# The softmax's row factors leave attention as rows in DRAM and are multiplied into the gates in the merge stage

## The reference

```python
logits = jnp.where(mask, scores + bias, -jnp.inf)     # 8 heads of width 64
p = jax.nn.softmax(logits, axis=-1)
att = jnp.einsum('bhqk,bkhd->bqhd', p, v)
y_b = att * jax.nn.silu(gbf)
merged = (gates[:, :, 0] * (y_a @ w_up_a) + gates[:, :, 1] * (y_b @ w_up_b)
          + gates[:, :, 2] * (y_c @ w_up_c))
out = merged @ w_out
return layer_norm(ALPHA * x + out, ln_g, ln_b)
```

## Time and profile before

| | |
|---|---|
| median of 3 timed runs | 1953.57 us (1952.46 to 1955.21) |
| profiled execution | 1956.44 us, its span 1954.8 us, mean TensorE clock 0.993 |
| TensorE busy | 1916.7 us (98%), 10560 matmuls |
| VectorE, ScalarE, GpSimd busy | 1125.0 us (58%), 708.7 us (36%), 435.1 us (22%) |
| attention | about 607 to 1577 us |
| merge | 1577 us to the end, a block each 44.6 us |

### The profile page before, as it was taken

The page is one execution under the profiler, slowest core; times in us unless marked ns, Lnnn a source line. Parts: engine busy times, 40 slices in busy tenths (PEclk is TensorE's granted clock), DMA queues, the critical chain, the costliest instruction groups (busy, mean ns, idle before and its releaser), DMA issues. The chain is left out here.

```text
span 1954.8 us, 30551 instructions
## 1 busy us (share of the span) xinstructions
PE 1916.7 (98%) x10560; PEld 1625.1 (83%) x10560; DVE 1125.0 (58%) x2142; ACT 708.7 (36%) x1090; POOL 435.1 (22%) x548
## 2 busy tenths in 40 slices
PE   7999999999999999999999999999999989999998
PEld 6878887888886888888888788888888878999997
DVE  4563235654244655646556665565655568777676
ACT  3121113021033554555555655455555541111110
POOL 1927940498000000000000000000000002222322
PEclk9999999999999999999999999999999989999999
DMA  6224225322432142241513515133142286555542
GB/s 187 65 91 117 89 86 193 66 97 109 138 120 87 56 124 68 66 125 48 138 54 89 186 50 139 54 89 109 48 136 66 87 262 208 167 174 170 174 118 87
DMA packets 105592, 221.69 MB, mean 113 GB/s; under 512 B 11000, under 2 KB 56744, under 8 KB 101928
## 3 DMA queue, kind: packets, MB, share of 16 engines
q1 hardware_dynamic: 92912, 165.61, 26.8%
q0 software_dynamic: 12608, 55.19, 10.2%
HBM read 155.09 MB, written 65.08 MB: 113 GB/s over the span
## 5 line engine op out<-in xcount | busy, mean ns | idle before, releaser
L1447 PE MATMUL g_ps<-x_hi,w_lo 128*128 128x512 f32 x768 | 309.7, 403 | 0.0
L1447 PE MATMUL g_ps<-x_hi,w_hi 128*128 128x512 f32 x768 | 308.2, 401 | 0.0
L1361 DVE TENSOR_TENSOR pt_lo<-t_ps,pt_hi 128x512 fp32r<-128x512 f32 (+2 forms) x320 | 191.7, 607 | 134.3 <-ACT pt_hi L1269 132.9
L1447 PE MATMUL g_ps<-x_lo,w_hi 128*128 128x512 f32 x768 | 228.1, 412 | 3.7 <-PEq L1484 2.7
L697 PE MATMUL tile_ps<-x_hi,w_hi 128*128 128x512 f32 x736 | 228.4, 391 | 1.5 <-DVE w_lo L379 1.5
L697 PE MATMUL tile_ps<-x_lo,w_hi 128*128 128x512 f32 x736 | 226.7, 389 | 0.0
L697 PE MATMUL tile_ps<-x_hi,w_lo 128*128 128x512 f32 x736 | 226.6, 389 | 0.0
L1269 ACT ACTIVATE pt_hi<-t_ps 128x512 fp32r<-128x512 f32 (+2 forms) x320 | 170.4, 534 | 135.0 <-PE t_ps L1406 130.6
L1177 POOL DMA_DIRECT2D mixT<-y_out x63 | 33.8, 536 | 749.4 <-DVE y_out L1315 749.4
L1301 DVE CUSTOM_DVE_ANT_0 s_sb<-s_ps,f_row 128x512 f32<-128x512 f32 (+2 forms) x320 | 180.7, 605 | 19.5 <-PE s_ps L1395 18.8
L1406 PE MATMUL t_ps<-ident,s_sb 128*128 128x128 f32 x1088 | 171.7, 273 | 1.6 <-DVE pt_lo L1361 1.0
(11 more groups left out here) (294 smaller groups left out, 3576.4 us busy)
## 6 DMA issues: line engine op xcount, KB each, us to landing
w_lo_raw<-in_w_tiles SPq DMA_DIRECT2D x96, 512.0 KB, 3.6
gateT<-g_out SPq DMA_DIRECT2D x96, 256.0 KB, 3.0
gate<-gateT SPq DMA_DIRECT2D x64, 384.0 KB, 4.5
qkvT<-zout SPq DMA_DIRECT2D x24, 512.0 KB, 3.2
x_lo_raw<-in_xT SPq DMA_DIRECT2D x20, 512.0 KB, 8.5
silT<-zout SPq DMA_DIRECT2D x16, 512.0 KB, 2.6
k_ll<-qkvT POOLq DMA_DIRECT2D x16, 512.0 KB, 7.4
q_st<-qkvT POOLq DMA_DIRECT2D x16, 512.0 KB, 9.1
```

The costliest lines, as they stand in the source:

```text
L1361: dve.tensor_tensor(pt_lo[part], t_ps[n % 2][:, 0:keys].rearrange("p (k q) -> p k q", q=P), pt_hi[part].bitcast(F32), ALU.subtract).then_i ...
L1447: mm = pe.matmul(g_ps[c][:], w[j % 2][:, k, :], x[:, k, c * BANK:(c + 1) * BANK], start=(r == 0), stop=(r == 3 * KT - 1))
```

## The change

The product stored to `mixT` is no longer divided by the row sums. `row_inv` is taken once for a head's 16 tiles (in the last head also once after tile 1), transposed once as [128 x 16] into 16 rows of `o_ps[:, 1]`, copied to `inv_row` (16 free partitions beside `y_out[0]`) and stored to a new scratch `inv` of 128 rows (head, tile) x 128 queries. GpSimd stores them after each head's last `y`; in the last head the first two rows go out after pair 0, and SP stores the rest after the last `y`. In merge `load_inv` brings a block's 256 factors of the four even heads to partitions 0 to 63 and of the four odd heads to 64 to 127, into the middle four of the eight slices of `y_lo`, which at that time is free. `split_y` multiplies `sil` of groups 1 and 2 (the attention rows) by them before the product with `mix`. The loads for block b+1 are issued by SP behind a wait for `lifted` of block b's last tile, as `y_lo` is read until then.

```diff
+        inv_row = kept.y_out[0][HD:HD + Q_TILES, 0:P]
@@ stage_attend, sync
-                        sp.wait_ge(y_stored, 16 * (HEADS * 8 - 7))
+                        sp.wait_ge(y_stored, 16 * ((HEADS - 1) * 9 + 2))
                         for g in range(YG):
+                            if g == 1:
+                                load_inv(sp, kept, scr, 0)
...
-            sp.wait_ge(y_ready, HEADS * 8)
+            sp.wait_ge(y_ready, HEADS * 9)
             row = (HEADS - 1) * HD + 2 * P
             sp.dma_start(scr["mixT"][row:row + HD, 14 * P:], y_out[1]).then_inc(last_y_stored, 16)
+            sp.wait_ge(y_ready, HEADS * 9 + 1)
+            sp.dma_start(scr["inv"][(HEADS - 1) * Q_TILES + 2:], inv_row[2:]).then_inc(last_y_stored, 16)
@@ gpsimd
+            def store_inv(h9, row, tiles, n):
+                pool.wait_ge(y_ready, h9 + n)
+                pool.dma_start(scr["inv"][bass.ds(row, tiles)], inv_row[0:tiles]).then_inc(y_stored, 16)
+                stored(h9 * 16 + 16 * n)
...
+                store_inv(h * 9, h * Q_TILES, Q_TILES, 9)
@@ vector
-            def output(at, p):
+            def output(at, p, last):
                 dve.wait_ge(o_low_ready, at(8, p + 1))
-                dve.wait_ge(y_free, at(8, p + 1))
-                y = y_out[p % 2]
-                dve.tensor_tensor(y[:], o_ps[0:HD, 0, :], o_low[:], ALU.add).then_inc(o_sum, 1)
-                dve.wait_ge(o_sum, at(8, p + 1))
-                dve.tensor_tensor(y[:], y[:], o_ps[0:HD, 1, :], ALU.mult).then_inc(y_ready, 1)
+                dve.wait_ge(y_free, at(9, p + (2 if last and p >= 3 else 1)))
+                dve.sem_inc(passed)
+                dve.tensor_tensor(y_out[p % 2], o_ps[0:HD, 0, :], o_low[:], ALU.add).then_inc(y_ready, 1)
+                if last and p == 0:
+                    dve.wait_ge(y_free, at(9, 2))
+                if p == 7 or (last and p == 0):
+                    dve.tensor_copy(inv_row, o_ps[0:Q_TILES, 1, 0:P]).then_inc(y_ready, 1)
...
-                    if t % 2 == 1:
+                    if t == Q_TILES - 1 or (last and t == 1):
                         dve.wait_ge(p_ready, at(Q_TILES, t + 1))
-                        dve.reciprocal(row_inv[:, t - 1:t + 1], row_sum[:, t - 1:t + 1]).then_inc(inv_ready, 1)
+                        dve.reciprocal(row_inv[:, 0:t + 1], row_sum[:, 0:t + 1]).then_inc(inv_ready, 1)
@@ tensor, values
-                pe.wait_ge(inv_ready, at(8, p + 1))
-                pe.sem_inc(passed)
-                for a in range(2):
-                    last = pe.transpose(o_ps[0:HD, 1, a * P:(a + 1) * P],
-                                        row_inv[:, 2 * p + a:2 * p + a + 1].broadcast_to([P, HD]), ident[:])
-                last.then_inc(o_full, 1)
+                if p == 7 or (final and p == 0):
+                    pe.wait_ge(inv_ready, at(1, 2 if final and p else 1))
+                    pe.sem_inc(passed)
+                    mm = pe.transpose(o_ps[0:Q_TILES, 1, 0:P], row_inv[:, 0:Q_TILES], ident[:])
+                mm.then_inc(o_full, 1)
@@ merge
+def load_inv(eng, kept, scr, b):
+    rows = scr["inv"].rearrange("(h t) q -> h (t q)", t=Q_TILES)
+    for odd in range(2):
+        eng.dma_start(kept.y_lo[odd * HD:(odd + 1) * HD, 2:6].bitcast(F32),
+                      rows[odd::2, bass.ds(b * BLOCK, BLOCK)].partition_broadcast(HD)).then_inc(kept.mix_loaded[1], 16)
+
 def split_y(dve, kept, b):
+    def scale(g):
+        dve.wait_ge(kept.mix_loaded[1], b * 64 + 64)
+        if g != 1:
+            dve.wait_ge(kept.mix_loaded[g], b * 32 + 32)
+        dve.tensor_tensor(kept.sil[g][:], kept.sil[g][:], group(kept.y_lo, g).bitcast(F32),
+                          ALU.mult).then_inc(kept.scaled, 1)
...
-    for g in range(YG):
-        dve.wait_ge(kept.mix_loaded[g], b * 32 + 32)
-        dve.tensor_tensor(kept.mix[g][:], kept.mix[g][:], kept.sil[g][:], ALU.mult).then_inc(kept.prod, 1)
-        if g:
-            finish(g - 1)
-    finish(YG - 1)
+    product(0)
+    scale(1)
+    scale(2)
+    finish(0)
+    product(1)
+    product(2)
+    finish(1)
+    product(3)
+    finish(2)
+    finish(3)
@@ stage_merge, sync
-            sp.wait_ge(kept.last_y_stored, 16)
+            sp.wait_ge(kept.last_y_stored, 32)
...
                 for d in range(KT):
+                    if d == KT - 1 and not last:
+                        sp.wait_ge(lifted, b * KT + KT)
+                        load_inv(sp, kept, scr, b + 1)
                     sp.wait_ge(m_split, b * KT + (d + 1))
```

More of the change, by code:

```diff
@@ L99, in __init__ @@
         self.g_out = [at(f"g_out{i}", 5, [P, BANK], skip=4 * i * BANK) for i in range(NCH)]
-        self.y_out = [at(f"y_out{i}", 5, [HD, 2 * P], skip=4 * (2 * BANK + i * 2 * P)) for i in range(2)]
+        self.y_out = [at(f"y_out{i}", 5, [P, 2 * P], skip=4 * (2 * BANK + i * 2 * P)) for i in range(2)]
         self.ln_g = at("ln_g", 5, [P, D])
@@ L1045, in stage_attend @@
         g_bias = sb("g_bias", [P, T_GATE])
-        g_out, y_out = kept.g_out, kept.y_out
+        g_out, y_out = kept.g_out, [y[0:HD] for y in kept.y_out]
+        inv_row = kept.y_out[0][HD:HD + Q_TILES, 0:P]
         k_hh = sb("k_hh", [P, S], F32R)
@@ L1172, in load_f, with stored, store_y @@
                 pool.dma_start(f_row[:], scr["fcum"][bass.ds(h, 1)].partition_broadcast(P)).then_inc(f_loaded, 16)
[L1174 to L1180 removed]
+            def stored(n):
+                pool.wait_ge(y_stored, n)
+                pool.sem_inc(y_free, 1)
+            def store_y(h9, row, p, more=0):
+                pool.wait_ge(y_ready, h9 + (p + 1 + more))
+                pool.dma_start(scr["mixT"][bass.ds(row, HD), p * 2 * P:(p + 1) * 2 * P],
+                               y_out[p % 2]).then_inc(y_stored, 16)
+                stored(h9 * 16 + 16 * (p + 1 + more))
+            def store_inv(h9, row, tiles, n):
+                pool.wait_ge(y_ready, h9 + n)
+                pool.dma_start(scr["inv"][bass.ds(row, tiles)], inv_row[0:tiles]).then_inc(y_stored, 16)
+                stored(h9 * 16 + 16 * n)
             pool.sem_inc(y_free, 2)
@@ L1353, in body @@
                     if t % 2 == 0 and t >= 2:
-                        output(at, t // 2 - 1)
-                    if t % 2 == 1:
+                        output(at, t // 2 - 1, last)
+                    if t == Q_TILES - 1 or (last and t == 1):
                         dve.wait_ge(p_ready, at(Q_TILES, t + 1))
-                        dve.reciprocal(row_inv[:, t - 1:t + 1], row_sum[:, t - 1:t + 1]).then_inc(inv_ready, 1)
+                        dve.reciprocal(row_inv[:, 0:t + 1], row_sum[:, 0:t + 1]).then_inc(inv_ready, 1)
                     for n, k0, keys in pieces(t):
@@ L1374, in body @@
                     split_kq(at(1, 2))
-                output(at, 7)
+                output(at, 7, last)
                 for j in splits("tail", last):
@@ L1419, in values, with head @@
                     for j, pt in enumerate((pt_hi, pt_lo)):
-                        pe.matmul(o_ps[:, 0, q], v_st[:, k, :], pt[:, k, q], start=(k == 0 and j == 0),
-                                  stop=(k == last_key and j == 1))
-                pe.wait_ge(inv_ready, at(8, p + 1))
-                pe.sem_inc(passed)
-                for a in range(2):
-                    last = pe.transpose(o_ps[0:HD, 1, a * P:(a + 1) * P],
-                                        row_inv[:, 2 * p + a:2 * p + a + 1].broadcast_to([P, HD]), ident[:])
-                last.then_inc(o_full, 1)
-            def head(at, phase):
+                        mm = pe.matmul(o_ps[:, 0, q], v_st[:, k, :], pt[:, k, q], start=(k == 0 and j == 0),
+                                       stop=(k == last_key and j == 1))
+                if p == 7 or (final and p == 0):
[3 more added lines that the diff above has]
+                mm.then_inc(o_full, 1)
+            def head(at, phase, final=False):
                     filled = [0]
@@ L1487, in _ @@
                     head(lambda k, c: i * k + (c + phase * PHASE_HEADS * k), phase)
-            head(lambda k, c: (HEADS - 1) * k + c, 1)
+            head(lambda k, c: (HEADS - 1) * k + c, 1, True)
 BLOCKS = S // BLOCK
@@ L1506, in group, with product @@
     return t[:, g * (KT // YG):(g + 1) * (KT // YG)]
-def split_y(dve, kept, b):
+def load_inv(eng, kept, scr, b):
[3 more added lines that the diff above has]
+                      rows[odd::2, bass.ds(b * BLOCK, BLOCK)].partition_broadcast(HD)).then_inc(kept.mix_loaded[1], 16)
+def split_y(dve, kept, b):
+    def scale(g):
[4 more added lines that the diff above has]
+                          ALU.mult).then_inc(kept.scaled, 1)
+    def product(g):
+        if g in (1, 2):
+            dve.wait_ge(kept.scaled, b * 2 + g)
+        else:
+            dve.wait_ge(kept.mix_loaded[g], b * 32 + 32)
+        dve.tensor_tensor(kept.mix[g][:], kept.mix[g][:], kept.sil[g][:], ALU.mult).then_inc(kept.prod, 1)
     def finish(g):
```

31 lines of the change are left out of this document (17 added, 14 removed).

## The result

The changed kernel takes 1976.55 us (median of 4 executions, 1975.59 to 1978.8) against 1953.01 us for the kernel before on the same chip: ratio 1.012, 95% interval 1.0107 to 1.0133. It is slower by 1.2%; forecast were 1945.0 us and 0.4% faster. Its profiled execution took 1975.59 us.

A forecast was written before the change was run, and what follows sets the result against it. The prediction took TensorE's matmul stream to bound attention (462.47 of 464 us busy). Its terms, -13.1 + 1.3 + 2.6 + 0.6 = -8.6 us, took 1953.57 to 1945.0 us; own range 1941 to 1948, wider range 1941 to 1951.

The forecast's parts named there:

- Attention: TensorE's stream in attention: 119 fewer transposes at 0.11 us each, -13.1 us, bounds about 11 and 15 us.
- the rest of attention: VectorE's relief, the new `y_free` wait and GpSimd's small stores in attention: 0 us each.
- rival B: In attention TensorE would wait for ScalarE and VectorE, giving back half of the 13.1 us: 1951.5 us; chance 10%.
- Passage into merge: Attention's end to merge's start: two more products and one more store issue, +1.3 us, bounds 0.6 and 2.0 us.
- They land before VectorE reaches them: At the passage into merge, the two factor loads arrive before VectorE's first product at 1569.53, costing 0 us.
- Block 0 to 1: First block change in merge, DMA saturated: two products +1.2 us, two loads +1.4 us, together 2.6 us, bounds 1.2 and 5.
- The clock: Longer TensorE gaps at two places could lengthen stretches at 1.2 GHz: 0.3 us each, 0.6 us in all.
- Blocks 1 to 6: Later merge blocks: factors issued near 1752.8 land by 1758.3, the new wait fits VectorE's idle 4.66 us: 0 us.
- a margin that the prediction put at 1.1 us: Blocks 1 to 6: room left before TensorE asks for the second gate product; hidden unless loads land later than about 6.5 us.
- rival A: Factor loads late in every merge block, holding VectorE's scaling, residual and first gate product: slower, 1960 us at 9 us; chance 8%.
- its own formula: Blocks 1 to 6: each microsecond of landing beyond about 6.5 us costs up to one, in six blocks; 9 us gives 15.
- the half of the ports: Skill's rule that 64 adjacent partitions reach half the DMA write ports, about 218 GB/s: sum 1.0 us higher at block 0 to 1.

The follow-up runs named there:

- attend_only: The changed kernel without the factor loads and without the two scaling products in merge; 1944.04 us, ratio 0.9949 to the kernel before.
- products_only: The changed kernel without the factor loads, the two scaling products kept with `sil` in place of the factors; 1947.0 us, ratio 0.9962 to the kernel before.
- distinct_rows: The changed kernel with the factor loads reading 64 different rows of `silT` in place of one row 64 times; 1975.75 us, ratio 1.0113 to before.
- long_rows: The changed kernel with factor loads reading one row of 4 KB for each partition in place of four of 1 KB; 1980.59 us, ratio 1.0144 to before.
- half_factors: The changed kernel loading two of the four slices of factors, 256 KB for 512; 1960.04 us, ratio 1.0033 to the kernel before.
- early_issue: The changed kernel with the factor pair issued once tile 7 is lifted, ahead of the gate loads of tiles 1 to 3; 1955.21 us, ratio 1.0007 to before.
- reorder: The changed kernel with VectorE doing groups 0 and 3, first residual and moments before scalings and groups 1 and 2; 1960.57 us, ratio 1.0037 to before.
- gates_later: The changed kernel with the gate loads of tiles 2 and 3 issued once the next block's `y` is split; 1963.79 us, ratio 1.0062 to before.

## Why the prediction was wrong

**Attention: right in mechanism, too large.** -13.1 us was forecast, with 11 as lower bound; measured from the first to the last gate-projection matmul, the changed kernel lies 10.3 us below before, attend_only 8.3, products_only 9.5, and the 15 traces with the change lie between 8.3 and 11.9. The cost of the transposes was right. From a pair's last value product to the next work, before and after:

```profile
888.21 0.28 PE L1420 MATMUL o_ps<-pt_lo,v_st 128*128 128x128 f32 x1
...
888.54 0.60 PE L1406 MATMUL t_ps<-ident,s_sb 128*128 128x128 f32 x4
```

```profile
884.11 0.28 PE L1442 MATMUL o_ps<-pt_lo,v_st 128*128 128x128 f32 x1
884.22 0.63 PE L1428 MATMUL t_ps<-ident,s_sb 128*128 128x128 f32 x4
```

That is 0.33 us and 0.11 us; summed over all 64 pairs it is 20.7 and 7.7 us, 13.0 less. What failed is that the rest of attention would stay as it was: 2.7 us come back elsewhere. The weight loads' waits of `t_ps` for `pt_lo` grew from 3.7 us in 9 to 7.1 in 15, which has the size. But in products_only they grew by 1.7 us with 3.6 missing, so what else takes the rest is open. It is rival B's direction at under half of its 6.5 us.

**Passage into merge: too small.** Forecast 1.3 us, gap 3.9; measured 4.6 us, gap 7.22. "They land before VectorE reaches them" held: the factors landed by 1557.1 and the first scaling began at 1561.44. What fails is the 0 behind it, for the loads that stand behind the factors: before, VectorE came to `sil` when it was there; now it waits 2.31 and 0.86 us for it. attend_only and products_only, without loads, have gaps of 3.5 and 3.9 us; distinct_rows, long_rows and half_factors, with loads, 3.8 and 3.9. So 0.5 MB in this place needn't cost it; why these factors do isn't shown.

**Block 0 to 1: right within its bounds.** Forecast 2.6 us (1.2 to 5), measured 1.0 + 3.1 = 4.1, of which block 1's share already holds a late factor load.

**The clock: not as forecast.** 0.6 us were put on longer stretches at 1.2 GHz around the two gaps. From 1565 to 1643, which holds both gaps, the trace has 13.7 us at that level both before and after. But two stretches of 3.4 us stand in blocks 6 and 7 of the changed kernel, where before has none at that place (the granted clock is 0.94 in the window 1874 to 1930, and was 1.00 from 1855 to 1912). At half speed they can hold up to 1.7 us each of what these two blocks lost.

**Blocks 1 to 6: this is the failed step.** "5 us gives 1758.3" and "So 0" took the landing from `sil`, "4.6 us there". Those loads weren't there: they were issued from 1759.5 to 1762.7, 6.7 us and more behind the place of the factors (1752.8). At that place the trace of before has the gate loads of 384 KB (issues, then issue to landing; `sil` second):

```profile
L1588 SPq DMA_DIRECT2D gate<-gateT x3: 372/372/373, 1750.5 to 1753.8; - x3
...
DMA to landing us min/median/max: 5.2/5.5/6.4
```

```profile
L1583 SPq DMA_DIRECT2D sil<-silT x4: 415/418/418, 1759.5 to 1762.7; - x4
...
DMA to landing us min/median/max: 3.3/4.6/5.2
```

Measured in block 3: 9.8 us from the first issue in place of 5.5, that is 4.3 us late, against a margin that the prediction put at 1.1 us. VectorE waited 8.63 us where the prediction had 4. The rest of the chain ran as described: scaling, nine operations, residual 5.8 us later (1767.35 to 1773.15), the GpSimd product on the gate add (2.50 us). The issue moved from 29.3 us into the block to 33.7 as a consequence, since the lift itself now takes 27.0 us; the pair then goes out 6.7 us after that lift's end, as the 6.5 us in the prediction's own picture (1746.31 to about 1752.8). Five block distances and the tail grew by 17.8 + 3.9 = 21.7 us. That is rival A, given 8%. The median landing of 8.1 us is past its threshold of 7.9, but by its own formula 8.1 us would have cost 6 x 1.6 = 9.6 us, just 1 us more than the gain. The formula took one load's landing; what counts is the pair's last landing from its first issue. With the 10 us measured for that, 6 x (10 - 6.5) = 21 us, which is the size found. Its 1960 us for 9 us was 16.6 us short: 6.7 of these are the blocks (21.7 for 15), 3.3 the gap, 2.8 attention and 1.5 block 0 to 1; the rest lies between executions.

For the half of the ports, the prediction held that only `k_ll` and `q_st` load over 64 partitions before. `vT` does too, 512 KB with a median of 4.7 us to landing against 7.4 for `k_ll`. This changes no term of the sum.

**What is shown and what isn't.** Shown: the loads alone carry the loss (products_only); it is undone by issuing them 10 us earlier in the block (early_issue) or by moving work in front of the wait (reorder), with the landing unchanged. Shown for blocks 1 to 6, with the neighbours in place: none of the repeated source address, the half of the partitions or the number of pieces makes the landing long by itself. Open: what does. No run has the pair without a gate load beside it, none tries other rows without neighbours, and `sil`'s 4.6 us come from another stretch of the block. early_issue, 10 us earlier, had the same 10 us for the pair; a stretch like `sil`'s was not tried.

## What to carry to other kernels

A load that can only be issued late because it borrows a buffer is priced by its issue place first: look at what the issuing queue is waiting for at that point (here a gate load's buffer, so that the pair went out 6.7 us behind the event that really freed its own), and move it ahead of that before accepting the change. Take the landing time from a load in the same stretch and of the same total bytes, counted from the first issue of the set to the last landing, and if the margin is one microsecond in a loop, give the rival more than a few per cent. If a wait can't be shortened, put the work that doesn't depend on it in front: here that brought the blocks back to 44.6 us with the landing unchanged.

## What the runs showed of the hardware

The transfer engines can be 93% busy and move 103 GB/s (the window of gates_later above), where in the earlier trace rows they move 355 GB/s at a share of 1.03: the busy share says little about what a further load will take. Widening a load from two times 64 to 128 partitions, or lengthening its pieces from 1 to 4 KB, changed nothing to its advantage in blocks 1 to 6 (51.8 and 58.5 us of waits for 53.0). Halving its bytes took 1 us off a landing of 8.1, and 2 us off the 10 from the pair's first issue to its last landing. At the end of attention, a pair of 2 x 256 KB from other rows landed in 4.4 and 4.5 us where the factors took 6.5 and 7.0 (distinct_rows).
